# First modulation by quarters of its columns, k projected block by block behind each quarter

## The reference, cut to what matters

```python
mod   = silu(c)     @ w_mod + b_mod        # 2048 -> 6 * 2048
mod_c = silu(c_ctx) @ w_mod + b_mod
sh1, sc1, ga1, sh2, sc2, ga2 = split(mod)  # csh1, csc1 of mod_c for the context
pc = (rmsnorm(ctx) * (1 + csc1) + csh1) @ w_in
p  = (rmsnorm(x)   * (1 + sc1)  + sh1)  @ w_in
# columns of p and pc: fourier | q, k | v | o | gates
```

## Time and profile before

| | us |
|---|---|
| median of 3 runs | 1950.05 (1948.74 to 1951.76) |
| the profiled execution | 1951.42 |
| its span, first to last instruction | 1949.5 |
| busy in it: TensorE / VectorE / ScalarE / POOL | 1609.5 / 1103.7 / 386.7 / 735.5 |

### The profile page before, as it was taken

How to read it: one execution, slowest core, us unless ns; L and a number is a source line. 1 busy time by engine, 2 the same in 40 slices (tenths; PEclk the granted TensorE clock), 3 DMA queues, 4 the chain that set the end, 5 groups by cost and what they waited for, 6 DMA issues and landing times.

```text
span 1949.5 us, 13823 instructions
## 1 busy us (share of the span) xinstructions
PE 1609.5 (83%) x4587; PEld 762.9 (39%) x4587; DVE 1103.7 (57%) x1850; ACT 386.7 (20%) x1142; POOL 735.5 (38%) x574
## 2 busy tenths in 40 slices
PE   3899999998999996999977777777777677777776
PEld 0346444556447872443433222232222222223332
DVE  1148783666566796343546466565665656646444
ACT  2011003124002002222212121221223212122112
POOL 1001000001000364656655554655537555455440
PEclk7899999999999997999999999999999999999999
DMA  9989775656984999999999999999999999999996
GB/s 379 407 315 336 271 279 191 213 200 241 368 293 179 413 418 422 423 422 422 423 422 422 423 422 422 423 422 423 422 422 422 423 423 422 422 422 422 423 422 251
DMA packets 139128, 725.72 MB, mean 372 GB/s; under 512 B 10602, under 2 KB 12874, under 8 KB 71987
## 3 DMA queue, kind: packets, MB, share of 16 engines
q0 software_dynamic: 92800, 614.83, 76.8%
q1 hardware_dynamic: 43888, 107.83, 14.9%
q10 hardware_dynamic: 2370, 2.19, 0.5%
HBM read 722.66 MB, written 2.15 MB: 372 GB/s over the span
## 4 chain that ended last, share of the span: by engine, by line
DMA 45%; PE 34%; DVE 11%; POOL 6%; issue 3%; SPq 1%; ACT 1%; DVEq 0%; POOLq 0%
DMA ring<-in_expert_v,acc 19%; PE ps L932 11%; DMA ring<-in_expert_u,acc 10%; PE ps L1198 8%; PE ps L1056 5%; DMA H<-in_expert_v,acc 4%; DMA modrow<-in_expert_v,acc 4%; DMA gwork<-in_expert_u,acc 3%; POOL ring L452 3%; DMA ring<-in_w_mod 2%; DMA VX<-in_expert_u,acc 2%; DMA qh<-in_expert_u,acc 1%; PE ps L839 1%; PE ps L926 1%; PE ps L928 1%
## 5 line engine op out<-in xcount | busy, mean ns | idle before, releaser
L1198 PE MATMUL ps<-ring,wg 128*128 128x512 f32 x1184 | 545.5, 607 | 165.9 <-DMA ring<-in_expert_v,acc 163.4
L1594 DVE SCALAR_TENSOR_TENSOR ring<-ring,A 128x2048 f32<-128x2048 f32 x135 | 307.7, 2292 | 290.6 <-DMA ring<-in_expert_u,acc 290.5
L1198 PEld LDWEIGHTS ps<-ring,wg 128*128 128x128 f32 x1184 | 218.0, 192 | 491.7 <-issue 312.5
L1198 PE MATMUL ps<-H,wg 128*128 128x512 f32 x576 | 262.2, 599 | 65.3 <-DMA H<-in_expert_v,acc 65.3
L452 POOL DMA_INDIRECT ring<-in_expert_v,acc x148 | 203.3, 1373 | 225.3 <-PE ps L1198 205.6
L757 ACT ACTIVATE wg<-K,VX 128x128 f32<-128x128 f32 x256 | 102.8, 402 | 653.0 <-PE ps L1198 651.5
L932 PE MATMUL ps<-ring,H 128*128 128x512 f32 x512 | 224.0, 597 | 2.2 <-ACT VX L565 2.2
L452 POOL DMA_INDIRECT ring<-in_expert_u,acc x135 | 180.7, 1339 | 91.8 <-DVE ring L1594 46.4
L1198 PEld LDWEIGHTS ps<-H,wg 128*128 128x128 f32 x576 | 104.8, 190 | 221.0 <-issue 135.3
L1223 DVE SCALAR_TENSOR_TENSOR acc<-ring,vec,acc 128x512 f32<-128x512 f32 x240 | 180.4, 752 | 15.3 <-DMA ring<-in_w_mod 7.0
L390 POOL DMA_DIRECT2D ring<-in_w_mod x32 | 28.5, 891 | 425.5 <-DVE acc L1223 325.0
(11 more groups left out here) (243 smaller groups left out, 1427.9 us busy)
## 6 DMA issues: line engine op xcount, KB each, us to landing
ring<-in_w_mod POOLq DMA_DIRECT2D x32, 2048.0 KB, 9.7
ring<-in_w_mod SPq DMA_DIRECT2D x16, 2048.0 KB, 21.8
ring<-in_w_in SPq DMA_DIRECT2D x15, 2048.0 KB, 13.7
ring<-in_w_query SPq DMA_DIRECT2D x8, 2048.0 KB, 14.2
ring<-in_w_out SPq DMA_DIRECT2D x12, 1024.0 KB, 9.1
ring<-in_expert_v,acc POOLq DMA_INDIRECT x148, 28.1
ring<-in_expert_u,acc POOLq DMA_INDIRECT x135, 28.8
B<-in_ctx SPq DMA_DIRECT2D x2, 1024.0 KB, 20.4
```

The costliest lines, as they stand in the source:

```text
L1198: ins = mm(ps[:, 4 * b + n, :], diag[:, r % 4, :], v_rows[r % V_SLOTS][:, n * CH:(n + 1) * CH], start=k == 0, stop=k == BLOCK_RANKS - 1, s ...
L1594: v.scalar_tensor_tensor(out=rows_u, in0=rows_u, scalar=1.0, in1=A[:, r // BLOCK_RANKS, :], op0=ALU.mult, op1=ALU.mult, accum_out=dots[:, ...
```

## The change

The first modulation's pieces are now quarters q: 512 shift columns and the same 512 scale columns, by 512 input channels, as two DMAs. After each quarter the scale and shift of four channel blocks are made. All 16 blocks of k are projected "early", one channel block over its four column groups at a time, with weights in KT, qh, gwork and gy, one of them loaded behind each quarter. One PSUM bank serves all transpositions. The gates are projected when k is complete, ahead of q. ctx and x are normed apart. POOL's load of gy waits until k is done.

```diff
@@ -96,16 +96,9 @@
-MODA_N, MODA_COLS, MODA_K = 4, 2 * CH, KB // 4
-MODA_BANKS = ((0, 1), (2, 3), (0, 6), (5, 0))
-MODA_AFTER = (1, 2, 3, 5)
-X_BANKS = (4, 5, 3, 4, 5, 3, 4, 5, 6, 5, 0, 6, 5, 0, 6, 5)
-X_BEFORE = (None, None, None, 0, 1, 2, 3, 4, None, None, None, 8, 9, 10, 11, 12)
+QUARTERS, MODA_K = 4, KB // 4
+MODA_BANKS = (0, 5)
+X_BANK = 6
...
-        WE = [KT[:], qh[:].rearrange("p a b t -> p (a b t)").rearrange("p (k n) -> p k n", k=4)]
+        WE = [KT[:], *(t.rearrange("p (k n) -> p k n", k=4) for t in (
+            qh[:].rearrange("p a b t -> p (a b t)"), gwork[:], gy[:]))]
         kraw = B[:, 0, :].rearrange("p (j t) -> p j t", j=4)
...
@@ -302,13 +296,20 @@
             wm, wi = w_mod[0], w_in[0]
 
             def load_moda(piece):
-                n, part = piece // 4, piece % 4
+                q, part = piece // 4, piece % 4
                 if piece >= 4:
                     sp.wait_ge(S["w_free"], piece - 3)
-                k0, n0 = part * MODA_K * P, moda_column(n)
-                sp.dma_start(WA[part], wm[k0:k0 + MODA_K * P, n0:n0 + MODA_COLS
-                                          ].rearrange("(k p) n -> p k n", p=P)
-                             ).then_inc(a_ld[part], 16)
+                k0 = part * MODA_K * P
+                for a in range(2):
+                    n0 = a * D + q * CH
+                    sp.dma_start(WA[part][:, :, a * CH:(a + 1) * CH], wm[k0:k0 + MODA_K * P, n0:n0 + CH
+                                                                         ].rearrange(
+                        "(k p) n -> p k n", p=P)).then_inc(a_ld[part], 16)
+
+            def load_early(q):
+                c0 = W_IN_CHUNKS[0] * CH
+                sp.dma_start(WE[q], wi[4 * q * P:4 * (q + 1) * P, c0:c0 + CH].rearrange(
+                    "(k p) n -> p k n", p=P)).then_inc(S["ld_we"], 16)
 
             load_moda(0)
...
                 sp.dma_start(tile[:, b, :], src[0, b * P:(b + 1) * P, :]).then_inc(S[loaded], 16)
                 if n < 4:
                     load_moda(n)
-            for piece in range(4, 8):
-                load_moda(piece)
-            c0 = W_IN_CHUNKS[0] * CH
-            for i in range(2):
-                sp.dma_start(WE[i], wi[4 * i * P:4 * (i + 1) * P, c0:c0 + CH].rearrange(
-                    "(k p) n -> p k n", p=P)).then_inc(S["ld_we"], 16)
-            for piece in range(8, 4 * MODA_N):
-                load_moda(piece)
-            sp.wait_ge(S["w_free"], 14)
-            load(1, wi, 1, bass.ds(W_IN_CHUNKS[0] * CH, CH))
+            load_early(0)
+            for q in range(1, QUARTERS):
+                for part in range(4):
+                    load_moda(4 * q + part)
+                load_early(q)
             for i, n in enumerate(W_IN_CHUNKS[1:], 1):
                 for kh in range(2):
-                    sp.wait_ge(S["w_free"], 16 + 2 * i + kh - 1 if (i, kh) != (1, 0) else 13)
+                    sp.wait_ge(S["w_free"], 16 + 2 * i + kh - 1 if i > 1 else 13 + kh)
                     load(kh, wi, kh, bass.ds(n * CH, CH))
 
             sp.wait_ge(S["w_free"], 32)
...
@@ -400,6 +396,7 @@
                         load(m, kh)
             load_from(1, MODB_SCAN + 1)
 
+            pool.wait_ge(S["w_free"], 18)
             pool.dma_start(gy[:, 0:FW], g_fourier.to_broadcast([P, FW])).then_inc(S["ld_gy"], 16)
             pool.dma_start(gy[:, FW:D], g_mlstm.to_broadcast([P, FW])).then_inc(S["ld_gy"], 16)
             load_from(MODB_SCAN + 1, MODB_LATE)
...
-            act.wait_ge(S["ssq"], 4)
-            nc_a.activation(st[:, 4:8], st[:, 0:4], ACT.Sqrt, bias=eps, scale=1.0 / D
-                            ).then_inc(S["std"], 1)
-
-
+                act.wait_ge(S["ssq"], 2 * (i + 1))
+                nc_a.activation(st[:, 4 + 2 * i:6 + 2 * i], st[:, 2 * i:2 * i + 2], ACT.Sqrt, bias=eps,
+                                scale=1.0 / D).then_inc(S["std"], 1)
             for k in range(0, KB, 2):
-                if k % KH == 0:
-                    act.wait_ge(S["mod_ready"], k // KH + 1)
+                act.wait_ge(S["mod_ready"], k // MODA_K + 1)
...
-            def partial_mod(n, part):
-                if part == 0:
-                    pe.wait_ge(S["moda_free"], MODA_AFTER[n])
-                pe.wait_ge(a_ld[part], 16 * (n + 1))
+            def partial_mod(q, part):
+                if part == 0 and q >= 1:
+                    pe.wait_ge(S["moda_free"], q)
+                pe.wait_ge(a_ld[part], 32 * (q + 1))
...
+            def columns_of_mod(q):
+                pe.wait_ge(S["moda_free"], q + 1)
+                if q >= 1:
+                    pe.wait_ge(S["mod_ready"], q)
+                for a in range(2):
+                    for k in range(MODA_K * q, MODA_K * (q + 1)):
+                        j = a * KB + k
+                        ins = mm(ps[:, 7, 2 * j:2 * j + 2], moda[:, j * P:(j + 1) * P], add4,
+                                 start=True, stop=True)
+                ins.then_inc(S["modcol_psum"], 1)
...
             def transpose_x(k):
-                if X_BEFORE[k] is not None:
-                    wait_ht(X_BEFORE[k])
+                if k >= 1:
+                    wait_ht(k - 1)
                 for b in range(4):
                     src = (B, A)[b // 2][:, b % 2, k * P:(k + 1) * P]
-                    ins = tr(ps[:, X_BANKS[k], b * P:(b + 1) * P], src, ident)
+                    ins = tr(ps[:, X_BANK, b * P:(b + 1) * P], src, ident)
                 ins.then_inc(S["xT_psum"], 1)
 
-            def project_early(first, last):
-
-                for step in range(first, last):
-                    j, k = step // KH, step % KH
-                    if j == 0:
-                        wait_ht(k)
-                    if step == 0:
-                        pe.wait_ge(S["ld_we"], 32)
+            def project_early(k):
+
+                if k % 4 == 0:
+                    pe.wait_ge(S["ld_we"], 16 * (k // 4 + 1))
+                wait_ht(k)
+                for j in range(4):
                     ins = mm(ps[:, 1 + j, :], WE[k // 4][:, k % 4, j * P:(j + 1) * P], H[:, k, :],
-                             start=k == 0, stop=False)
-                    if step == 4 * KH - 1:
-                        ins.then_inc(S["w_free"], 1)
+                             start=k == 0, stop=k == KB - 1)
+                if k >= KB - 2:
+                    ins.then_inc(S["w_free"], 1)
 
             pe.wait_ge(S["vecz_ready"], 1)
-            for n in range(2):
-                for part in range(4):
-                    partial_mod(n, part)
+            for part in range(4):
+                partial_mod(0, part)
             pe.wait_ge(S["ld_const"], 16)
             columns_of_mod(0)
             pe.wait_ge(S["xn_ready"], 4)
             transpose_x(0)
-            transpose_x(1)
-            columns_of_mod(1).then_inc(S["modcol_psum"], 1)
-            transpose_x(2)
-            partial_mod(2, 0)
-            for k in range(3, 6):
-                transpose_x(k)
-            partial_mod(2, 1)
-            for k in range(6, 8):
-                transpose_x(k)
-            project_early(0, 4)
-            partial_mod(2, 2)
-            project_early(4, 8)
-            partial_mod(2, 3)
-            project_early(8, 12)
-            pe.wait_ge(S["mod_ready"], 1)
-            columns_of_mod(2)
-            partial_mod(3, 0)
-            project_early(12, 15)
-            partial_mod(3, 1)
-            project_early(15, 18)
-            partial_mod(3, 2)
-            project_early(18, 21)
-            partial_mod(3, 3)
-            transpose_x(8)
-            project_early(21, 24)
-            columns_of_mod(3).then_inc(S["modcol_psum"], 1)
-            transpose_x(9)
-            transpose_x(10)
-            project_early(24, 26)
-            for k in range(11, 14):
-                transpose_x(k)
-                project_early(15 + k, 16 + k)
-            transpose_x(14)
-            project_early(29, 31)
-            transpose_x(15)
-            project_early(31, 32)
+            for q in range(QUARTERS):
+                k, more = MODA_K * q, q + 1 < QUARTERS
+                if more:
+                    partial_mod(q + 1, 0)
+                transpose_x(k + 1)
+                project_early(k)
+                if more:
+                    partial_mod(q + 1, 1)
+                    partial_mod(q + 1, 2)
+                transpose_x(k + 2)
+                project_early(k + 1)
+                if more:
+                    partial_mod(q + 1, 3)
+                transpose_x(k + 3)
+                project_early(k + 2)
+                if more:
+                    columns_of_mod(q + 1)
+                    transpose_x(k + 4)
+                project_early(k + 3)
...
-                pe.wait_ge(w_ld[kh], 16 * (i + kh))
+                pe.wait_ge(w_ld[kh], 16 * i)
...
-                        gate_parts_of_projection()
-                    if (i, kh, j) == (0, 1, 1):
+                    if (i, kh, j) == (1, 0, 0):
                         sum_gates()
```

(68 more changed lines are left out.)

44 lines of the change are left out of this document (7 added, 37 removed).

## The result

| us | before | after |
|---|---|---|
| median, runs in alternation | 1950.76 (1948.74 to 1952.49, 6 runs) | 1957.51 (1956.74 to 1959.08, 6 runs) |
| the profiled execution | 1951.42 | 1959.08 |
| its span | 1949.5 | 1957.4 |

The ratio is 1.0037, with the interval [1.0027, 1.0048]: the changed kernel is slower by 6.8 us, where +4.1 was predicted. The profiled execution after is the slowest of its six runs.

A forecast was written before the change was run, and what follows sets the result against it. Bound: a load of w_mod until 70.71, then TensorE alone; after the change VectorE is last at row sum 0. Row sum 0 +1.8 and clock +2.3 make 4.1 us: 1950.05 + 4.1 = 1954.2, range 1947.5 to 1960.5.

The forecast's parts named there:

- main step: At row sum 0: TensorE arrives 10.8 us earlier, then idles 12.6 us waiting for VectorE's delayed second modulation.
- The loads and the start: Start of the kernel: w_mod pieces land every 5.4 us, x 1.1 us later, piece 4 at 48.0; x is normed by 46.9.
- Block 15: Last modulated block of k: leaves VectorE at 136.8, not 126.12; bounds 132.2 to 140.
- VectorE is late: Second modulation ahead of row sum 0: 62.9 us shift whole, m = 2 ends 1.7 later; row sum 0 +1.8.
- The wait costs twice: Behind row sum 0: after idling 12.6 us TensorE also loses clock, +2.3 us.
- Not late a second time: At the second row_out: VectorE is there at 286.3, TensorE lets it go at 288.5, so no second wait.
- The sum: Whole kernel: 4.1 us later, median 1954.2, on the line of about 0.2% (3.9 us) between slower and no change.
- likeliest case: VectorE last at row sum 0: +2 to +7 us, time 1952 to 1957, chance 0.50.
- rival C: First modulation's loads: short runs of w_mod come at 5.8 us a piece, block 15 at 140.5; +8, time 1958; chance 0.14.
- A: Second modulation: POOL's loads run ahead and VectorE's 6.7 us of waits go; -5 to -7, time 1944.5; chance 0.08.
- B: Row sum 0 at 199 to 200: block 15 at 134.5 or m = 2 loads miss SP's; 0 to +2, 1951.5; chance 0.26.
- D: Early k: columns don't start before 70 us as piece 4 or x come late; block 15 at 150, time 1965; chance 0.02.

The follow-up runs named there:

- c1: The changed kernel, but SP's first load for v waits until q is projected (w_free 20, not 19): 1958.34, ratio 1.0041.
- e3: The changed kernel with 16 matmuls that nobody reads ahead of the wait in row sum 0: 1955.86, ratio 1.0024.
- e1: The changed kernel with ROW_SUM_BEHIND = [19, 29], so row sum 0 stands two groups of matmuls later: 1951.10, ratio 1.0003.
- b2: The kernel before, with VectorE's second modulation held until the gates' sum is done: 1967.65, ratio 1.0085.
- e4: The changed kernel with each w_mod piece as one DMA of 1024 adjacent columns (scale's columns wrong): 1957.35, ratio 1.0030.
- a0: The changed kernel itself, run again in later rounds: 1960.57, ratio 1.0054.
- b1: The kernel before, with VectorE's second modulation held until the gates' matmuls are done: 1960.19, ratio 1.0050.
- e4b: The changed kernel with one DMA of 1024 adjacent columns a w_mod piece, run again in later rounds: 1956.66, ratio 1.0031.
- e8: The changed kernel with the first half of VectorE's second modulation done ahead of the last block's modulation: 1949.15, ratio 0.9995.

## Why the prediction was right, and where its sizes were off

The prediction's main step held: the kernel becomes slower because TensorE's gain of 11.5 us ends in a wait for VectorE's `m_free` 8, whose start the change delays. Point by point:

- **The loads and the start.** Pieces 5.42 us apart (5.4 predicted); piece 4 landed at 48.13 (48.0), x at 40.00, squares from 40.02 (39.9), the first transposition at 47.08 (46.9). Piece 6 was awaited for 1.8 us, not 0.4.
- **Block 15.** VectorE started at 136.27 (136.8), k was complete at 142.12 (142.8), and the gates at 145.7 (146.4). TensorE stood at the row sum at 188.17 (188.9). Half a microsecond early all along. A piece takes 5.42 us in runs of 512 columns (2 KB) and 5.12 in runs of 1024 (4 KB), which is 5.9% more. The Trainium skill ("DMA: Bandwidth & Descriptors", "Why small descriptors are slow (HBM only)") counts 3 fixed cycles to each packet, from which 2 KB runs would be 2.3% slower, an estimate. The traces show more than twice that.
- **VectorE is late.** This is the term that was too small: 62.9 + 1.7 was predicted for the stretch, 62.9 + 3.7 measured. The two loads of m = 2 took 8.8 and 11.2 (9.2 and 10.8 assumed), which was about right. What failed stands ahead of them: the prediction let the loads of m = 1 land as before, but the second one took 9.7 us where it had taken 8.5. These are the two issues, at 149.21 in the changed kernel and at 139.06 in the kernel before:

```profile
ring<-in_w_mod POOLq DMA_DIRECT2D x1, 2048.0 KB, 9.7
ring<-in_w_mod POOLq DMA_DIRECT2D x1, 2048.0 KB, 8.5
```

So the second half of m = 1 waited for 1.61 us and not for 0.46, and the last load of m = 2 was issued 1.2 us later than the start of 136.27 alone explains, at 165.90. Together with SP's load beside it this made the second half of m = 2 wait for 4.25 us, where it had waited for 0.66; only the first half of m = 2 waited for less (1.72, before 2.78). SP's load was not beside the load of 149.21: SP's next one was issued at 160.66, and in c1, where it comes at 174.44, the load still took 9.5. Why it took longer stays open. Row sum 0 stands at +3.2 and not +1.8.
- **The wait costs twice.** TensorE idled for 14.7 and not 12.6 us, and the clock cost 2.9 and not 2.3, by e3.
- **Not late a second time.** Right as predicted for this kernel (1.77 us behind TensorE). In e1, where TensorE does not lose its time at the first row sum, VectorE is late at the second by 8.40. In the changed kernel VectorE was done 8.8 us ahead there (280.6 against 289.44) only because TensorE came 16.5 us later than in e1.
- **The sum.** 3.2 + 2.9 = 6.1 at 304 us, where 4.1 was predicted. The rest of the 6.8 lies behind it and I leave it open: in single traces the end of the span is later against before than the scores are by -0.7 (b2) to +2.7 us (c1), about as much as runs of one kernel spread. The median of 1957.51 lies just above the likeliest case's own range (1952 to 1957). As a number it is nearer to rival C's 1958 than to the forecast of 1954.2, but C's cause did not come about.
- **The rivals.** A did not come about: the waits for loads grew, they did not go. Nor did B: block 15 was only 0.5 us earlier than predicted, and the loads of m = 2 met SP's. C's mechanism is real at 5.42 and not 5.8 us a piece. D did not come about: k columns ran from 52.36.
- **Two slips in the working.** By the prediction's own shift of 10.7 us POOL's loads of m = 2 would be issued at 158.5 and 165.2, not at 158.3 and 164.7, and by its own prices one piece, the columns and four and a half blocks are 21.0 us, not 20.5. Neither changes the forecast.

## What to carry to other kernels

When the bound engine is made faster, work out the slack of every engine it waits for later, and compare it with the gain plus the delay of that engine's own start: here 10.7 us of slack stood against 11.5 of gain, 10.2 of delay and 3.7 of longer waits, and the sum, 14.7, is the idle time. Then move the place of the wait together with the change: one pair of numbers (`ROW_SUM_BEHIND`) was worth 17 us (1957.5 to 1940.8). And follow it to the next wait of the same kind, since the first one hides the second (e1).

## What the runs showed of the hardware that was not expected

- Two loads of 2 MB issued within 0.3 us of each other on two queues took 14.3 us each; with none of SP's beside it such a load took 8.3 (c1) to 9.7 us (changed kernel, at 149.21) from issue to landing, partly overlapped 8.8 and 11.2.
- A load of 2 MB from w_mod landed every 5.12 us in runs of 4 KB and every 5.42 in runs of 2 KB. A load of w_in in runs of 2 KB took 5.4 as a single DMA (e4).
- The idle of 2.2 us ahead of the o columns (ACT VX L559) was followed by 32 matmuls of 15.67 us in before, after, a0, b1, b2, e3, e4 and e4b and of 13.97 in e1, e8 and c1, with the same idle of 2.19. The 1.7 us are the clock: before was granted 0.53 from 300.4 to 304, e8 1.00 from 296.8 on. What decides whether the clock falls there stays open.
